# Crossing between stages of a two-layer decoder trunk: passes with a wait for each half, and the last tile transposed into another pair of PSUM banks

## The chip, the cores and the metric

The kernel runs on one core of a Trainium2 chip. The metric is the device time of one execution in microseconds; the median over a few runs counts. The engines are named as the profile names them: PE is TensorE (PEld its weight loads), ACT is ScalarE, DVE is VectorE, POOL is GpSimd, SP is SyncE, which issues most of the DMAs.

## The reference, cut to what matters

A decoder trunk of two layers over 512 tokens with width 1024, all in float32. For each layer i:

```
hn = rms_norm(x, g0);  y = attention_i(hn)          # layer 0 differential, layer 1 native sparse
x = x + rms_norm(y, g1)
hn = rms_norm(x, g2);  u = hn @ w_up                # 1024 -> 5632
c = causal depthwise convolution of u over 3 tokens; gate, val = split(c)
f = (gelu(gate) * val) @ w_down                     # 2816 -> 1024
x = x + rms_norm(f, g3)
x = x + sigmoid(rms_norm(x, g4) @ gate_w) * (p[i] @ proj_w)
```

Native sparse attention compresses keys and values in blocks, attends to the compressed, the selected and the window keys, and adds the three with learned gates. In each sublayer the normalised x is the input of a matrix product, so it must be there transposed (features on the partitions).

## The kernel before, in words

**Splitting.** Every product in float32 is made of three passes of the fast float32r matmul: a value is split into a high part (`_hi`, rounded to float32r) and a low part (`_lo`, the rest), and hi x hi, hi x lo and lo x hi are added up in one PSUM bank. This holds for the weights (`w_hi`, `w_lo`) and for the normalised, transposed x (`nT_hi`, `nT_lo`).

**Weights.** They come in 213 units of 128 x 1024 (512 KB), in the order of use, listed in `PLAN`. For each unit SP loads `w_raw`, ACT copies it to `w_hi` (L356, `w_high`), POOL subtracts to `w_lo` in four parts (L295, `low`), and PE uses it. Each has a ring of four slots. A slot of `w_hi` is free when PE has counted the unit in `units_done`; `w_hi_done` counts the units that ACT has made, `w_lo_done` the quarters that POOL has made. On PE `weights(u)` waits for all quarters of the units before u.

**Tiles.** The 512 tokens are four tiles of 128. PSUM has eight banks of 512 columns, four called A and four called B. A stage that ends with an update of x (attention output, down projection, gate) runs its last units tile by tile (`by_tile`), so that tile 0's x is ready while PE is still at work on the later tiles.

**From one stage to the next.** For the q-th normalisation and for each tile t: ACT makes the sums of squares and the root, DVE writes the normalised tile into the one buffer `xn` in two halves (L785, `prepare`; it waits until the tile before has been transposed), PE transposes it with eight matmuls into two banks (L1179, `transposes`; `xT_banks` names the banks, B[0] and B[1] for every tile), ACT copies them rounded to `nT_hi` (L389) and DVE subtracts to `nT_lo` (L791), which frees the two banks. `xn_done`, `xT_done`, `nhi_done` and `nlo_done` count the halves, 8 for each q. DVE's order at the end is fixed: update of tile 3, `xn` of tile 3, `nT_lo` of tile 2, `nT_lo` of tile 3 (`turns`).

**The crossing.** `transposes(q, 0)` and `(q, 1)` stand inside the last stage's `by_tile`. `cross` is the start of the next stage on PE: it waits for `nT_lo` of tiles 0 and 1 and the first unit's `w_lo`, runs unit 0 on tiles 0 and 1 (`part(0, 0)`), transposes tile 2, waits for `w_lo`, runs unit 1 on tiles 0 and 1, transposes tile 3, runs unit 2 on tiles 0 and 1, then waits for all of `nT_lo` and runs the three units on tiles 2 and 3. It is called five times: into up0 (q = 1), gate0a (2), cmp (3), up1 (4) and gate1a (5). In up0, up1 and cmp a part is `features` over half of the columns, 24 matmuls of 256 columns (L1200) with the weights as stationary operand; in gate0a and gate1a it is `of_tiles` with two tiles, 12 matmuls of 512 columns (L1209) with x as stationary operand. Bank A[n] takes unit n in the first case, bank A[t] tile t in the second.

**After the crossing.** In up0 and up1 units of 24 matmuls follow in a loop. After gate0a and gate1a come two units `ple`, which need `pe_hi` and `pe_lo`: ACT loads `pe_raw` (issued in `embed`, behind the loads of `gains`, which wait for `nlo_done`), copies it and then makes the weights of the ple units.

Of the kernel before, what the change touches and what calls it, by code (L numbers as in the profile page):

```python
# [37 lines left out]
SEQ = 512  # L38
D = 1024
TT = SEQ // P  # L40
KT = D // P
# [26 lines left out]
RING = 4  # L68
# [54 lines left out]
def trunk(nc, x_in, w_in, const_in, gain_in, conv_in, subln_in, lam_in, pos_in, pT_in, w1_in,  # L123
          cpos_in, w2_in, out):
    ctx = ExitStack()
    with ctx:
        def sb(name, shape, dt=F32, on=ctx):
            return on.enter_context(nc.sbuf_tensor(name, shape, dt))
# [3 lines left out]
        nT_hi = sb("nT_hi", [P, KT, SEQ], F32R)  # L132
        nT_lo = sb("nT_lo", [P, KT, SEQ], F32R)
# [88 lines left out]
        A, B = [banks_a[:, n, :] for n in range(4)], [banks_b[:, n, :] for n in range(4)]  # L222
# [17 lines left out]
        S = {n: ctx.enter_context(nc.semaphore(n)) for n in names}  # L240
        block = ctx.enter_context(nc.Block())

        def tok(t):
            return slice(t * P, (t + 1) * P)
# [6 lines left out]

        def xT_banks(q, t):

            return ((A[0], A[1]), (A[2], A[3]), (B[0], B[1]), (B[2], B[3]))[t] if q == 0 else (B[0], B[1])

        def normed(q, t):

            return xn0[:, t, :] if q == 0 else xn[:, :]
# [82 lines left out]
        def _(act):  # L341
# [44 lines left out]
            def nT_high(q, t):  # L386
                for b, bank in enumerate(xT_banks(q, t)):
                    act.wait_ge(S["xT_done"], 8 * q + 2 * t + b + 1)
                    signal(act.activation(nT_hi[:, 4 * b:4 * b + 4, tok(t)],  # L389
                                          bank.rearrange("p (k n) -> p k n", k=4), ACT.Copy),  # L390
                           "nhi_done", 8 * q + 2 * t + b + 1)
# [375 lines left out]
        def _(dve):  # L767
# [20 lines left out]
            def nT_low(q, t):  # L788
                for b, bank in enumerate(xT_banks(q, t)):
                    dve.wait_ge(S["nhi_done"], 8 * q + 2 * t + b + 1)  # L790
                    signal(dve.tensor_tensor(nT_lo[:, 4 * b:4 * b + 4, tok(t)],  # L791
                                             bank.rearrange("p (k n) -> p k n", k=4),
                                             nT_hi[:, 4 * b:4 * b + 4, tok(t)].bitcast(F32), ALU.subtract),
                           "nlo_done", 8 * q + 2 * t + b + 1)
# [378 lines left out]
        def _(pe):  # L1173
            def weights(u):

                pe.wait_ge(S["w_lo_done"], u * PARTS)

            def transpose(dst, src):
                return pe.matmul(dst, src, ident[:, :], start=True, stop=True, is_transpose=True)  # L1179

            def transposes(q, t):

                if q and t:
                    pe.wait_ge(S["nlo_done"], 8 * q + 2 * t)
                for b, bank in enumerate(xT_banks(q, t)):
                    pe.wait_ge(S["xn_done"], 8 * q + 2 * t + b + 1)
                    for k in range(4):
                        m = transpose(bank[:, k * P:(k + 1) * P], normed(q, t)[:, (4 * b + k) * P:(4 * b + k + 1) * P])
                    m.then_inc(S["xT_done"], 1)

            def features(bank, slot, rhs_hi, rhs_lo, part=None, cols=slice(0, SEQ)):


                steps = [(k, pas) for k in range(KT) for pas in range(3)]
                if part is not None:
                    steps = steps[8 * part:8 * part + 8]
                for k, pas in steps:
                    w = (w_hi, w_hi, w_lo)[pas][slot]
                    r = (rhs_hi, rhs_lo, rhs_hi)[pas]
                    m = pe.matmul(bank[:, cols], w[:, k * P:(k + 1) * P], r[:, k, cols], start=(k, pas) == (0, 0),  # L1200
                                  stop=(k, pas) == (KT - 1, 2))
                return m

            def tokens(bank, slot, c, lhs_hi, lhs_lo, kk, t, n_k):

                for pas in range(3):
                    w = (w_hi, w_lo, w_hi)[pas][slot]
                    a = (lhs_hi, lhs_hi, lhs_lo)[pas]
                    m = pe.matmul(bank[:, :], a[:, kk, tok(t)], w[:, c * HALF:(c + 1) * HALF],  # L1209
                                  start=(kk, pas) == (0, 0), stop=(kk, pas) == (n_k - 1, 2))  # L1210
                return m

            def by_unit(U, units, banks, lhs_hi, lhs_lo, n_k, before=None):

                for n in units:
                    weights(U + n + 1)
                    if before:
                        before(n)
                    of_tiles(U, n, range(TT), banks, lhs_hi, lhs_lo, n_k).then_inc(S["units_done"], 1)

            def of_tiles(U, n, tiles, banks, lhs_hi, lhs_lo, n_k):

                for c in range(2):
                    kk = 2 * n + c - (n_k if 2 * n >= n_k else 0)
                    for t in tiles:
                        m = tokens(banks[t], (U + n) % RING, c, lhs_hi, lhs_lo, kk, t, n_k)
                return m

            def by_tile(U, units, banks, lhs_hi, lhs_lo, n_k, within, at, free=None):


                for t in range(TT):
                    if free:
                        free(t)
                    for n in units:
                        if t == 0:
                            weights(U + n + 1)
                        if n == units[at]:
                            within(t)
                        m = of_tiles(U, n, (t,), banks, lhs_hi, lhs_lo, n_k)  # L1240
                        if t == TT - 1:
                            m.then_inc(S["units_done"], 1)
                    if t < TT - 1:
                        m.then_inc(S["tile_done"], 1)

            def cross(U, q, part):


                pe.wait_ge(S["nlo_done"], 8 * q + 4)
                weights(U + 1)  # L1250
                part(0, 0)
                transposes(q, 2)
                weights(U + 2)
                part(1, 0)
                transposes(q, 3)
                weights(U + 3)
                part(2, 0)
                pe.wait_ge(S["nlo_done"], 8 * q + 8)
                for n in range(3):
                    part(n, 1).then_inc(S["units_done"], 1)  # L1260

            def feature_part(U):
                return lambda n, m: features(A[n], (U + n) % RING, nT_hi, nT_lo, cols=slice(256 * m, 256 * m + 256))

            def feature_start(U, q):

                cross(U, q, feature_part(U))
                weights(U + 4)
                features(A[3], (U + 3) % RING, nT_hi, nT_lo).then_inc(S["units_done"], 1)
# [27 lines left out]

            def embed(layer, q, after_q):
                Ua, Up, Ub = PLAN[f"gate{layer}a"], PLAN[f"ple{layer}"], PLAN[f"gate{layer}b"]
                cross(Ua, after_q, lambda n, m: of_tiles(Ua, n, (2 * m, 2 * m + 1), A, nT_hi, nT_lo, KT))  # L1300
                by_unit(Ua, (3,), A, nT_hi, nT_lo, KT)
                pe.wait_ge(S["pelo_done"], layer + 1)
                for half, banks in enumerate((B, A)):
                    weights(Up + half + 1)
                    for t in range(TT):
                        if half:
                            pe.wait_ge(S["sig_done"], 8 * layer + t + 1)
                        for c in range(2):
                            m = tokens(banks[t], (Up + half) % RING, c, pe_hi, pe_lo, c, t, 2)
                    m.then_inc(S["units_done"], 1)  # L1310

                def free(t):
                    pe.wait_ge(S["xhalf_done"], 4 * layer + t + 1)

                def within(t):
                    if q is not None and t >= 2:
                        if t == 2:
                            pe.wait_ge(S["sig_done"], 8 * layer + 6)
                        transposes(q, t - 2)
                by_tile(Ub - 4, range(4, 8), B, nT_hi, nT_lo, KT, within, 2, free)  # L1320
# [4 lines left out]
            for t in range(TT + 1):  # L1325
                if t < TT:
                    transposes(0, t)
                if t:
# [3 lines left out]
                    for n in range(2):  # L1332
                        m = of_tiles(PLAN["v"], n, (t - 1,), A, nT_hi, nT_lo, KT)
# [105 lines left out]
            mlp(0, "up0", 1)  # L1439
            down(0, "down0", 2, 1)  # L1440
            embed(0, 3, 2)


            feature_start(PLAN["cmp"], 3)
            U = PLAN["branch"]
# [15 lines left out]
            for t in range(TT):  # L1461
                m = transpose(A[3][:, tok(t)], gT[:, tok(t)])
# [151 lines left out]
            mlp(1, "up1", 4)  # L1614
            down(1, "down1", 5, 3)
            embed(1, None, 5)


# [103 lines left out]
```

## Time and profile before

| | |
|---|---|
| median of 3 runs | 1533.87 us (1533.52 to 1535.57) |
| the profiled execution, own time | 1532.11 us |
| its span | 1530.3 us |
| PE busy | 1467.9 us (96%) |
| DVE / ACT / POOL busy | 718.1 / 717.3 / 677.4 us |
| granted PE clock, mean | 0.991 of full speed |

The busy time of an engine is the sum over its instructions; PE's matmuls are pipelined, so the pace is read from the starts of neighbouring matmuls and not from their durations. In the timeline a row gives start, length, engine, line, operation, output and inputs, shapes and count, and in brackets how long the engine sat idle before it and what released it. Neighbouring rows of one kind are drawn together: "x8" is eight instructions in one row.

### The profile page before, as it was taken

Reading aid. Unit: us, or ns where it says so; the run is one execution under the profiler, and the core shown is the slowest. Engines: PE = TensorE matmul, PEld = TensorE weight load, DVE = VectorE, ACT = ScalarE, POOL = GpSimd, SP = SyncE. Lnnn points to the kernel's source line nnn. Section 1 sums busy time; section 2 is a strip of 40 time slices with the busy share of each in tenths; the row PEclk is TensorE's granted clock in tenths of the full one; section 3 lists DMA queues with packets and bytes.
Section 4 is the critical chain, followed back from the end, with each engine's and each line's share of the span. In section 5 each row is a group of like instructions: output and inputs, shape, how many; then the busy total and the mean of one; then the engine's idle time right before and its main releaser. Section 6 shows DMA issues by size and latency. Waiting matters only on the chain.

```text
span 1530.3 us, 23460 instructions
## 1 busy us (share of the span) xinstructions
PE 1467.9 (96%) x7566; PEld 1222.1 (80%) x7566; DVE 718.1 (47%) x1256; ACT 717.3 (47%) x1305; POOL 677.4 (44%) x970
## 2 busy tenths in 40 slices
PE   6999979999999999998999999999999999999998
PEld 5877757888888888877978787878788888888876
DVE  5477772644444400335476767673634443410053
ACT  5245543654444413357365656463744444423252
POOL 4634434365656555363420202112455656555452
PEclk9999998999999999999999999999999999999999
DMA  5321111232222222142410101010232222232221
GB/s 206 117 68 55 55 42 58 94 108 98 96 96 96 96 96 97 69 145 78 160 45 13 55 15 41 14 41 28 71 123 96 96 96 96 96 103 91 96 96 55
DMA packets 37131, 126.22 MB, mean 82 GB/s; under 512 B 6096, under 2 KB 6864, under 8 KB 36816
## 3 DMA queue, kind: packets, MB, share of 16 engines
q1 hardware_dynamic: 31824, 115.88, 21.6%
q10 hardware_dynamic: 5248, 9.55, 1.8%
q8 instruction: 37, 0.61, 0.2%
q14 instruction: 22, 0.18, 0.0%
HBM read 123.32 MB, written 2.10 MB: 82 GB/s over the span
## 4 chain that ended last, share of the span: by engine, by line
PE 58%; issue 17%; POOL 16%; DVE 5%; ACT 4%; POOLq 0%; ACTq 0%; DVEq 0%
PE banks_a L1200 22%; POOL w_lo L295 15%; PE banks_b L1209 9%; PE banks_a L1209 8%; PE banks_a L1564 4%; PE banks_b L1200 4%; PE banks_a L1179 4%; PE banks_b L1536 2%; PE banks_b L1356 1%; PE banks_a L1375 1%; DVE nm L938 1%; PE banks_b L1179 1%; PE banks_a L1455 1%; ACT w_hi L356 1%; ACT y L359 0%
## 5 line engine op out<-in xcount | busy, mean ns | idle before, releaser
L295 POOL TENSOR_TENSOR w_lo<-w_raw,w_hi 128x256 fp32r<-128x256 f32 x852 | 647.9, 793 | 776.7 <-ACT w_hi L356 776.6
L1200 PE MATMUL banks_a<-nT_hi,w_hi 128*128 128x512 f32 (+1 forms) x968 | 365.5, 378 | 1.6 <-POOL w_lo L295 1.6
L1200 PE MATMUL banks_a<-nT_lo,w_hi 128*128 128x512 f32 (+1 forms) x968 | 364.0, 376 | 0.0
L1200 PE MATMUL banks_a<-nT_hi,w_lo 128*128 128x512 f32 (+1 forms) x968 | 363.4, 375 | 0.0
L356 ACT ACTIVATE w_hi<-w_raw 128x1024 fp32r<-128x1024 f32 x213 | 225.6, 1061 | 284.5 <-PE banks_b L1209 137.9
L1200 PEld LDWEIGHTS banks_a<-nT_hi,w_hi 128*128 128x128 f32 x968 | 183.7, 190 | 34.2 <-POOL w_lo L295 1.8
L1200 PEld LDWEIGHTS banks_a<-nT_hi,w_lo 128*128 128x128 f32 x968 | 183.6, 190 | 32.0
L1200 PEld LDWEIGHTS banks_a<-nT_lo,w_hi 128*128 128x128 f32 x968 | 183.8, 190 | 31.7
L844 DVE SCALAR_TENSOR_TENSOR y<-banks_a,conv,y 128x511 f32<-128x511 f32 x88 | 66.0, 750 | 220.4 <-ACT y L457 219.9
L457 ACT ACTIVATE y<-banks_a,conv 128x512 f32<-128x512 f32 x88 | 68.6, 779 | 208.8 <-PE banks_a L1200 208.7
L938 DVE TENSOR_REDUCE nm<-banks_b 128x2 f32<-128x256 f32 (+2 forms) x96 | 79.1, 824 | 25.3 <-PE banks_b L1359 12.7
L691 ACT ACTIVATE gp<-banks_b,nm 128x128 f32<-128x128 f32 (+3 forms) x128 | 67.6, 528 | 49.1 <-DVE nm L938 43.4
L1564 PE MATMUL banks_a<-Vg,gpT 128*128 128x128 f32 x640 | 84.6, 280 | 0.0
L802 DVE TENSOR_TENSOR y<-banks_b,g_post 128x512 f32<-128x512 f32 x16 | 11.1, 692 | 143.7 <-ACT y L359 143.7
L1564 PEld LDWEIGHTS banks_a<-Vg,gpT 128*128 128x128 f32 x640 | 76.5, 192 | 0.3
L846 DVE SCALAR_TENSOR_TENSOR y<-banks_a,conv,y 128x510 f32<-128x510 f32 x88 | 65.8, 748 | 12.1
L1209 PE MATMUL banks_a<-w_hi,hT_hi 128*128 128x512 f32 x176 | 69.1, 393 | 0.0
L1209 PE MATMUL banks_a<-w_hi,hT_lo 128*128 128x512 f32 x176 | 68.5, 389 | 0.0
L1209 PE MATMUL banks_a<-w_lo,hT_hi 128*128 128x512 f32 x176 | 68.5, 389 | 0.0
L1209 PE MATMUL banks_b<-w_hi,hT_hi 128*128 128x512 f32 x176 | 68.5, 389 | 0.0
L1209 PE MATMUL banks_b<-w_lo,hT_hi 128*128 128x512 f32 x176 | 68.5, 389 | 0.0
L1209 PE MATMUL banks_b<-w_hi,hT_lo 128*128 128x512 f32 x176 | 68.5, 389 | 0.0
(256 smaller groups left out, 2405.6 us busy)
## 6 DMA issues: line engine op xcount, KB each, us to landing
w_raw<-in_w SPq DMA_DIRECT2D x213, 512.0 KB, 3.2
g_pre<-in_gains ACTq DMA_DIRECT2D x6, 512.0 KB, 6.0
x<-in_x SPq DMA_DIRECT2D x4, 512.0 KB, 9.6
g_post<-in_gains ACTq DMA_DIRECT2D x4, 512.0 KB, 6.9
out<-x SPq DMA_DIRECT2D x4, 512.0 KB, 2.6
pe_raw<-in_pT ACTq DMA_DIRECT2D x2, 512.0 KB, 5.6
w1k<-in_w ACTq DMA_DIRECT2D x1, 1024.0 KB, 4.9
w1v<-in_w ACTq DMA_DIRECT2D x1, 1024.0 KB, 7.0
```

Source lines behind the costliest of these rows:

```text
L295: pool.tensor_tensor(w_lo[slot][:, cols], w_raw[k % RAW][:, cols], w_hi[slot][:, cols].bitcast(F32), ALU.subtract).then_inc(S["w_lo_done"], 1)
L356: act.activation(w_hi[u % RING][:, :], w_raw[u % RAW][:, :], ACT.Copy).then_inc(S["w_hi_done"], 1)
L457: signal(act.activation(dst, bank[:, :], ACT.Identity, bias=conv[:, bass.ds(4 * f + 3, 1)], scale=conv[:, bass.ds(4 * f + 2, 1)]), "aff_do ...
L691: signal(act.activation(gp[:, k % 2, c, 0:n], B[2 * (k % 2) + c][:, 0:n], ACT.Exp, bias=nm[:, qt, c:c + 1], accum_out=sums[:, h % 2, qt, c ...
L844: link(dve.scalar_tensor_tensor(dst[:, 1:SEQ], bank[:, 0:SEQ - 1], conv[:, bass.ds(4 * f + 1, 1)], dst[:, 1:SEQ], ALU.mult, ALU.add))
L846: last = dve.scalar_tensor_tensor(dst[:, 2:SEQ], bank[:, 0:SEQ - 2], conv[:, bass.ds(4 * f, 1)], dst[:, 2:SEQ], ALU.mult, ALU.add)
L938: signal(dve.tensor_reduce(nm[:, qt, :], banks_b[:, b:b + 2, 0:n], AX.X, ALU.max, negate=True), negmax, step + 1)
L1179: return pe.matmul(dst, src, ident[:, :], start=True, stop=True, is_transpose=True)
L1200: m = pe.matmul(bank[:, cols], w[:, k * P:(k + 1) * P], r[:, k, cols], start=(k, pas) == (0, 0), stop=(k, pas) == (KT - 1, 2))
L1209: m = pe.matmul(bank[:, :], a[:, kk, tok(t)], w[:, c * HALF:(c + 1) * HALF], start=(kk, pas) == (0, 0), stop=(kk, pas) == (n_k - 1, 2))
L1536: pe.matmul(B[2 * (k % 2) + c][:, 0:n], Q[h][:, tok(qt)], K[:, c, 0:n], start=K is Kh, stop=False)
L1564: m = pe.matmul(A[c][:, tok(qt)], gpT[:, k % 2, c, kb * P:(kb + 1) * P], Vg[:, kb, HEAD * c:HEAD * c + P], start=kb == 0, stop=kb == qt)
```

## The change

The diff has three parts. `xT_banks` gives tile 3 the banks B[2] and B[3] for q > 0, and `transposes` drops tile 3's wait for `nlo_done` (tiles 0 to 2 keep theirs). `features`, `tokens` and `of_tiles` take a list of passes; with it the three passes no longer alternate within a unit, but each pass runs over the whole part. `cross` calls its parts pass by pass: pass 0 (hi x hi) after waits on `w_hi_done` and `nhi_done`, pass 1 (high weights with `nT_lo`) after `nlo_done`, pass 2 (`w_lo`) after `weights`. The parts on tiles 2 and 3 run in the same order of passes without waits in between.

```diff
         def xT_banks(q, t):
-            return ((A[0], A[1]), (A[2], A[3]), (B[0], B[1]), (B[2], B[3]))[t] if q == 0 else (B[0], B[1])
+            if q == 0:
+                return ((A[0], A[1]), (A[2], A[3]), (B[0], B[1]), (B[2], B[3]))[t]
+            return (B[2], B[3]) if t == TT - 1 else (B[0], B[1])
...
             def transposes(q, t):
-                if q and t:
+                if q and t < TT - 1:
                     pe.wait_ge(S["nlo_done"], 8 * q + 2 * t)
...
-            def features(bank, slot, rhs_hi, rhs_lo, part=None, cols=slice(0, SEQ)):
+            def features(bank, slot, rhs_hi, rhs_lo, part=None, cols=slice(0, SEQ), passes=None):
                 steps = [(k, pas) for k in range(KT) for pas in range(3)]
...
+                if passes is not None:
+                    steps = [(k, pas) for pas in passes for k in range(KT)]
...
-            def tokens(bank, slot, c, lhs_hi, lhs_lo, kk, t, n_k):
-                for pas in range(3):
+            def tokens(bank, slot, c, lhs_hi, lhs_lo, kk, t, n_k, passes=range(3)):
+                for pas in passes:
...
             def cross(U, q, part):
-                pe.wait_ge(S["nlo_done"], 8 * q + 4)
-                weights(U + 1)
-                part(0, 0)
+                def first_tiles(n):
+                    pe.wait_ge(S["w_hi_done"], U + n + 1)
+                    part(n, 0, (0,))
+                    if n == 0:
+                        pe.wait_ge(S["nlo_done"], 8 * q + 4)
+                    part(n, 0, (1,))
+                    weights(U + n + 1)
+                    part(n, 0, (2,))
+                pe.wait_ge(S["nhi_done"], 8 * q + 4)
+                first_tiles(0)
                 transposes(q, 2)
-                weights(U + 2)
-                part(1, 0)
+                first_tiles(1)
                 transposes(q, 3)
-                weights(U + 3)
-                part(2, 0)
+                first_tiles(2)
                 pe.wait_ge(S["nlo_done"], 8 * q + 8)
                 for n in range(3):
-                    part(n, 1).then_inc(S["units_done"], 1)
+                    part(n, 1, (0, 1, 2)).then_inc(S["units_done"], 1)
...
-                cross(Ua, after_q, lambda n, m: of_tiles(Ua, n, (2 * m, 2 * m + 1), A, nT_hi, nT_lo, KT))
+                cross(Ua, after_q, lambda n, m, passes: of_tiles(Ua, n, (2 * m, 2 * m + 1), A, nT_hi, nT_lo, KT,
+                                                       sorted((0, 2, 1)[pas] for pas in passes)))
```

In `tokens` the passes are numbered differently (1 is the one with `w_lo`), which is what the `(0, 2, 1)` translates.

## Rows read from the trace of the kernel before

**Rows 1.** The page: busy time and instructions of the engines; one group of loads.
```profile
PE 1467.9 (96%) x7566; PEld 1222.1 (80%) x7566; DVE 718.1 (47%) x1256; ACT 717.3 (47%) x1305; POOL 677.4 (44%) x970
...
L1200 PEld LDWEIGHTS banks_a<-nT_hi,w_hi 128*128 128x128 f32 x968 | 183.7, 190 | 34.2 <-POOL w_lo L295 1.8
```

**Rows 2.** Waits of PE: us in total, times, longest.
```profile
PE banks_b L1179 <- DVE nT_lo L791: 9.8, 5, 3.8
...
PE banks_a L1200 <- POOL w_lo L295: 1.6, 3, 0.7
```

**Rows 3.** Timeline of PE over the crossing into up0: start, us, what.
```profile
286.21 0.28 PE L1200 MATMUL banks_a<-nT_hi,w_hi 128*128 128x256 f32 x1
...
289.08 1.04 PE L1179 MATMUL banks_b<-ident,xn 128*128 128x128 f32 x8
290.84 0.39 PE L1200 MATMUL banks_a<-nT_hi,w_hi 128*128 128x256 f32 x1 [0.72 <-POOL w_lo L295]
...
295.26 1.09 PE L1179 MATMUL banks_b<-ident,xn 128*128 128x128 f32 x8 [1.29 <-DVE nT_lo L791]
296.11 0.36 PE L1200 MATMUL banks_a<-nT_hi,w_hi 128*128 128x256 f32 x1
```

**Rows 4.** Timeline of POOL and DVE over the same crossing.
```profile
287.01 10.22 POOL L295 TENSOR_TENSOR w_lo<-w_raw,w_hi 128x256 fp32r<-128x256 f32 x12 [1.54 <-ACT w_hi L356]
...
291.69 2.20 DVE L785 SCALAR_TENSOR_TENSOR xn<-x,rinv,g_pre 128x512 f32<-128x512 f32 x2
293.81 1.40 DVE L791 TENSOR_TENSOR nT_lo<-banks_b,nT_hi 128x512 fp32r<-128x512 f32 x2
296.66 1.42 DVE L791 TENSOR_TENSOR nT_lo<-banks_b,nT_hi 128x512 fp32r<-128x512 f32 x2 [1.45 <-ACT nT_hi L389]
```

**Rows 5.** Timeline over the crossing into gate0a: xn of tile 3, unit 2.
```profile
657.99 2.19 DVE L785 SCALAR_TENSOR_TENSOR xn<-x,rinv,g_pre 128x512 f32<-128x512 f32 x2
...
662.41 0.48 PE L1209 MATMUL banks_a<-w_hi,nT_hi 128*128 128x512 f32 x1
```

**Rows 6.** Timeline over the crossing into cmp: xn of tiles 2 and 3.
```profile
716.34 1.93 DVE L785 SCALAR_TENSOR_TENSOR xn<-x,rinv,g_pre 128x512 f32<-128x512 f32 x2
...
718.74 0.36 PE L1200 MATMUL banks_a<-nT_hi,w_hi 128*128 128x256 f32 x1
...
722.83 1.42 DVE L785 SCALAR_TENSOR_TENSOR xn<-x,rinv,g_pre 128x512 f32<-128x512 f32 x2
...
725.62 1.97 PE L1179 MATMUL banks_b<-ident,xn 128*128 128x128 f32 x8 [3.77 <-DVE nT_lo L791]
...
727.24 0.56 PE L1200 MATMUL banks_a<-nT_hi,w_hi 128*128 128x256 f32 x1
...
728.66 0.28 PE L1200 MATMUL banks_a<-nT_hi,w_hi 128*128 128x256 f32 x1
```

**Rows 7.** Crossing into up1: timeline; one stretch, its third last column the granted clock.
```profile
1103.26 2.19 DVE L785 SCALAR_TENSOR_TENSOR xn<-x,rinv,g_pre 128x512 f32<-128x512 f32 x2
...
1106.83 1.35 PE L1179 MATMUL banks_b<-ident,xn 128*128 128x128 f32 x8 [1.97 <-DVE nT_lo L791]
1107.84 0.56 PE L1200 MATMUL banks_a<-nT_hi,w_hi 128*128 128x256 f32 x1
...
1110.96 0.28 PE L1200 MATMUL banks_a<-nT_hi,w_lo 128*128 128x256 f32 x1
...
1109.00:1111.00 2.00, 2.00 (x12) 2.00 (x11) 0.67 (x1) 0.00 (x0) 0.00 (x0) 0.52 0.74 248
```

**Rows 8.** Timeline over the crossing into gate1a: xn of tile 3, unit 2.
```profile
1471.09 2.20 DVE L785 SCALAR_TENSOR_TENSOR xn<-x,rinv,g_pre 128x512 f32<-128x512 f32 x2
...
1475.51 0.47 PE L1209 MATMUL banks_a<-w_hi,nT_hi 128*128 128x512 f32 x1
```

**Rows 9.** Timeline of POOL and PE at the first unit of ple0.
```profile
675.45 2.84 POOL L295 TENSOR_TENSOR w_lo<-w_raw,w_hi 128x256 fp32r<-128x256 f32 x4 [11.93 <-ACT w_hi L356]
...
678.84 0.39 PE L1209 MATMUL banks_b<-w_hi,pe_hi 128*128 128x512 f32 x1
```

More of the change, by code:

```diff
@@ L1219, in by_unit, with of_tiles @@
                     of_tiles(U, n, range(TT), banks, lhs_hi, lhs_lo, n_k).then_inc(S["units_done"], 1)
-            def of_tiles(U, n, tiles, banks, lhs_hi, lhs_lo, n_k):
+            def of_tiles(U, n, tiles, banks, lhs_hi, lhs_lo, n_k, passes=range(3)):
                 for c in range(2):
@@ L1225, in of_tiles @@
                     for t in tiles:
-                        m = tokens(banks[t], (U + n) % RING, c, lhs_hi, lhs_lo, kk, t, n_k)
+                        m = tokens(banks[t], (U + n) % RING, c, lhs_hi, lhs_lo, kk, t, n_k, passes)
                 return m
@@ L1246, in cross @@
             def cross(U, q, part):
-                pe.wait_ge(S["nlo_done"], 8 * q + 4)
-                weights(U + 1)
-                part(0, 0)
+                def first_tiles(n):
[8 more added lines that the diff above has]
+                first_tiles(0)
                 transposes(q, 2)
-                weights(U + 2)
-                part(1, 0)
+                first_tiles(1)
                 transposes(q, 3)
-                weights(U + 3)
-                part(2, 0)
+                first_tiles(2)
                 pe.wait_ge(S["nlo_done"], 8 * q + 8)
                 for n in range(3):
-                    part(n, 1).then_inc(S["units_done"], 1)
+                    part(n, 1, (0, 1, 2)).then_inc(S["units_done"], 1)
             def feature_part(U):
-                return lambda n, m: features(A[n], (U + n) % RING, nT_hi, nT_lo, cols=slice(256 * m, 256 * m + 256))
+                return lambda n, m, passes: features(A[n], (U + n) % RING, nT_hi, nT_lo,
+                                                     cols=slice(256 * m, 256 * m + 256), passes=passes)
             def feature_start(U, q):
```

## The prediction

> **What bounds the kernel now.** I read the page's busy table first, then TensorE's waits, then the timeline of each place where the kernel goes from one stage to the next. TensorE (PE) is busy 96% of the span [rows 1]; what it is not busy for is the only thing to win. Among its waits the two that matter here are "transposes of tile 3 wait for nT_lo", 9.8 us in 5 waits, and "first matmul of a new stage waits for w_lo", 1.6 us in 3 waits of the L1200 stages [rows 2]. Both sit at the five crossings of `cross` (into up0, gate0a, cmp, up1, gate1a, at about 286, 652, 714, 1097 and 1465 us); from there the next stage keeps PE fed, so a microsecond won at a crossing is carried to the end. I found no idle of PE over 0.25 us inside the up and down stages.
>
> The crossing into up0 shows the pattern [rows 3]. Unit 0 on tiles 0 and 1 runs from 286.21 to 289.08: 24 matmuls of 256 columns, 0.12 us each, 2.87 us. Eight transposes follow at 289.08. Then PE sits 0.72 us until unit 1's w_lo is there and restarts at 290.84. Unit 1 takes 2.9 us; then PE sits 1.29 us until 295.26, when tile 3 may be transposed, and restarts with unit 2 at 296.11. What it waits for is the bank: DVE writes tile 3's xn at 291.69 to 293.89, then reads tile 2 out of banks B0 and B1 at 293.81 to 295.21 (nT_lo), and only that lets tile 3's transposes into the same two banks [rows 4].
>
> **The change part by part.**
>
> *Tile 3 into B2 and B3.* It takes the nT_lo wait away. What is late next is xn of tile 3, which nothing in the change moves: it hangs on the last tile's statistics, and its own write waits only for tile 2's transposes. How soon does unit 2 restart after xn's end? Crossing three has the case already, at tile 2: xn ends at 716.34 + 1.93 = 718.27 and the matmul behind the transposes starts at 718.74, 0.47 us later [rows 6]; the first four transposes are done before the second half of xn ends. So the new restart is xn's end + 0.47:
> up0: 293.89 + 0.47 = 294.36 against 296.11, 1.75 us saved [rows 3, 4];
> gate0a: 660.18 + 0.47 = 660.65 against 662.41, 1.76 us [rows 5];
> cmp: 724.25 + 0.47 = 724.72 against 727.24, 2.52 us [rows 6];
> up1: 1105.45 + 0.47 = 1105.92 against 1107.84, 1.92 us [rows 7];
> gate1a: 1473.29 + 0.47 = 1473.76 against 1475.51, 1.75 us [rows 8].
> Sum 9.70 us. Before the restart PE is free in each case: in up0 unit 1 would end near 293.0.
>
> *Pass by pass with a wait for each half.* The first pass (w_hi with nT_hi) needs no w_lo, so unit 1 starts directly behind tile 2's transposes: 0.85 to 1.1 us earlier in four crossings (290.84 against about 289.9 in up0), and unit 0 of cmp 0.3 us earlier. Its third pass comes 1.9 us later, and w_lo was there 0.1 us before the old restart. But nearly all this time is swallowed, for unit 2 restarts by xn, as above. What the passes give beyond that is PE's readiness: in up0 unit 1 would otherwise end at 290.84 + 2.88 = 293.72 and tile 3's first four transposes (0.44 us) at 294.2 instead of 293.94, 0.25 us late. So some 0.2 us of the 1.75 in up0, gate0a and gate1a are theirs, 0.6 us in all; the other 9.1 belong to the banks. The matmuls are the same in number and shape. The waits added are on w_hi and nT_hi, which were there over a microsecond before; behind PE's waits nothing else is queued but PE itself. I take 0, with bounds of 0 and 0.05 us for each of some 8 added waits in 5 crossings, 2 us.
>
> *The wait for tiles 2 and 3, `nlo_done` 8q+8.* DVE now goes from nT_lo of tile 2 straight to tile 3 without its 1.45 us pause: 295.21 + 1.46 = 296.67 in up0 [rows 4]. PE is then in unit 2 until 294.36 + 2.95 = 297.31. The cover is 0.6 us (0.5 in the gate stages, where a part has 12 matmuls of 512 columns). I take 0.
>
> *The clock.* In cmp and up1 the long wait is followed by slow matmuls. After 3.77 us idle the six matmuls from 727.24 to 728.66 take 1.42 us where six at full pace take 0.80; after 1.97 us idle fourteen from 1107.84 to 1110.96 take 3.12 us where 1.76 is the full pace, and the granted clock from 1109 to 1111 is 0.52, the 1.2 GHz level [rows 6, 7]. After the waits of 1.29 us (up0) and of 1.4 us in the gate stages there is no slow stretch. The change leaves in up1 about 0.6 us idle, four transposes, 0.7 us idle; I expect full clock and add 3.12 - 1.76 = 1.36 us. In cmp PE ends unit 1 at 721.85 and finds xn's first half at 723.6, 1.8 us idle, close to the case that fell. If the clock stays up, cmp gains another 1.42 - 0.80 = 0.62 us; if it falls, I price the slow stretch as up1's, 1.36 us. I take the middle of +0.62 and 0.62 - 1.36 = -0.74: -0.1 us.
>
> *What follows gate0a.* The first weights of ple0: w_lo ends at 675.45 + 2.84 = 678.29, and PE asks at 678.84 [rows 9], 0.55 us of cover for 1.76 us of advance. That w_lo hangs on ACT, whose pe_raw load is issued after nlo_done of the crossing, which moves ahead by 1.42 us. 0.55 + 1.42 - 1.76 = 0.21 us left over; bounds 0 and, if the load's landing stays put, 1.21 us lost. I take 0.2 us lost, for the advance may not pass through the queue whole.
>
> Sum: 9.70 + 1.36 - 0.1 - 0.2 = 10.8 us. The profiled execution took 1532.11 us (span 1530.3, 1.8 us around it); 1532.1 - 10.8 = 1521.3. The median of the runs shown is 1533.87, 1.8 us above the profiled one; since times after will be a median too, the forecast is 1533.87 - 10.8 = **1523.1 us**.
>
> **The rivals.**
> A. *The clock falls all the same* in cmp and in up1. For: the half-speed stretch in up1 came after only 1.97 us of idle, so that it may come after 0.6 + 0.7 with transposes between; against: 0.72 + 1.29 us in up0 did not bring it. It takes 1.36 + 0.64 us off: 8.8 us, 1525.1.
> B. *DVE becomes the bound.* PE now arrives at `nlo_done` 8q+8 0.5 to 0.6 us behind DVE. If tile 3's nT_lo operations were stretched as xn is (1.1 us for one of the two instead of 0.7, while GpSimd runs beside them), four in a row would be 1.6 us longer and PE would wait 1.0 us at each crossing, 5 us in all; with the ple0 cover gone too, 1.0 more: gain 4.8 us, 1529.1. Against: nT_lo at 293.81 ran at 0.70 us each beside GpSimd [rows 4].
> C. *Slower: the pass order costs pace.* In the old order of `features` two matmuls in succession use the same stationary operand (w_hi[k] with nT_hi and nT_lo), in the new one none do. If a load stops being hidden, each matmul costs up to the load's own 0.19 us instead of 0.12: 0.07 x 24 matmuls x 6 parts x 3 stages = 30 us, and with the gain taken off 19 us slower, 1553. It decides from 0.025 us per matmul (10.8 / 432). For: nothing in the trace has ever run in this order. Against: there are as many loads as matmuls, 7566 of each [rows 1], and 968 for each of the three passes at the same 190 ns [rows 1], so nothing was shared before. "TensorE: Matmul & The Clock Gate" of the Trainium skill (section "Step-by-step: what each phase is for") says that the load is its own instruction so that one load can serve many matmuls, which would speak against splitting the pair. The same page of the Trainium skill (section "LDWEIGHTS (loading the stationary operand)") gives columns / 1.2 ns for a load, 107 ns for 128 columns, which would still fit under 0.12 us; by that figure the order costs nothing.
> D. *It does nothing.* If xn's second half were late enough to hold PE as long as nT_lo does; the rows have xn 1.4 us before nT_lo's end in all five, so this needs xn to move. 0 us, 1533.9.
>
> **How the numbers follow.** Forecast with the clock saved in up1: 0.76. A 0.13, B 0.05, C 0.03, D 0.03. Own range of the forecast: cmp's clock either way (0.7 us), an added low-clock stretch or one fewer elsewhere (1.4 us, the price of one), the ple0 cover (1.0) and about 1 us of spread between medians (the three runs lie 1533.52 to 1535.57): 1520 to 1526.5. To reach A's far side I extend to 1527.5. A difference of less than 0.2% (3.1 us) can't be told from none. Faster by more: forecast, A, B, 0.94; same: D, 0.03; slower: C, 0.03.
>
> **What would show it.** Right: PE's wait for nT_lo before L1179 gone from all five crossings and a wait for xn of about 0.6 us in its place; the first matmul of unit 2 0.47 us behind xn; no PE wait for w_lo at the crossings; nT_lo of tiles 2 and 3 in one unbroken run of four. Wrong: a wait of PE for nT_lo before a matmul of L1200 or L1209 (B), matmuls of 256 columns further apart than 0.12 us at full clock (C), a granted clock near 0.5 after 1104 us (A), or the stages after a crossing taking back what it gave.

## The result

| | median | runs | ratio to before, 95% interval |
|---|---|---|---|
| before | 1533.52 us | 5 (1531.07 to 1535.57) | |
| changed | 1524.09 us | 5 (1522.84 to 1525.07) | 0.9936 [0.9925, 0.9948] |

The change makes the kernel 9.4 us faster by the medians (forecast 10.8, 1523.1 us); the interval of the ratio is 8.0 to 11.5 us. The profiled execution of the changed kernel took 1524.09 us (span 1522.3), 8.0 us less than that of before.

PE's waits in the changed kernel (us in total, times, longest) answer to [rows 2]:

```profile
PE banks_b L1181 <- DVE xn L787: 4.6, 7, 1.8
...
PE banks_a L1213 <- POOL w_lo L297: 2.5, 1, 2.5
...
PE banks_b L1213 <- POOL w_lo L297: 0.5, 2, 0.3
PE banks_b L1213 <- DVE x L874: 0.5, 1, 0.5
```

The 9.8 us for nT_lo are gone. In their place stand 4.6 us for xn in seven waits, six of them under 0.5 us and one of 1.77 us in cmp. The 2.5 us for w_lo are the very first units of the kernel, at 17.7 us; no wait for w_lo is left in `cross`. Behind gate0a one wait is new, 0.32 us for w_lo, and one has grown: PE's wait for x took 0.16 us before and takes 0.47 us now.

The crossing into up0, PE and DVE (start, us, what), answers to [rows 3, 4]:

```profile
287.72 1.11 PE L1204 MATMUL banks_a<-nT_hi,w_hi 128*128 128x256 f32 x8
288.67 1.12 PE L1204 MATMUL banks_a<-nT_lo,w_hi 128*128 128x256 f32 x8
...
294.33 0.64 PE L1181 MATMUL banks_b<-ident,xn 128*128 128x128 f32 x4
295.45 0.66 PE L1181 MATMUL banks_b<-ident,xn 128*128 128x128 f32 x4 [0.48 <-DVE xn L787]
295.86 0.36 PE L1204 MATMUL banks_a<-nT_hi,w_hi 128*128 128x256 f32 x1
...
293.19 2.21 DVE L787 SCALAR_TENSOR_TENSOR xn<-x,rinv,g_pre 128x512 f32<-128x512 f32 x2
295.32 2.86 DVE L793 TENSOR_TENSOR nT_lo<-banks_b,nT_hi 128x512 fp32r<-128x512 f32 x4
```

xn ends at 293.19 + 2.21 = 295.40, the second four transposes start at 295.45, unit 2 at 295.86: 0.46 us behind xn. nT_lo of tiles 2 and 3 is one run of four and ends at 295.32 + 2.86 = 298.18; PE starts the parts on tiles 2 and 3 at 298.82, 0.64 us later. Eight matmuls of one pass take 288.67 - 287.72 = 0.95 us, 0.119 us each, the pace of before. Unit 2 starts at 660.39, 1102.98 and 1467.52 in gate0a, up1 and gate1a, 0.46 to 0.47 us behind xn each time (the first two are shown). In cmp, where the clock fell, it is 0.95 us (the rows stand with e10).

```profile
657.73 2.19 DVE L787 SCALAR_TENSOR_TENSOR xn<-x,rinv,g_pre 128x512 f32<-128x512 f32 x2
...
660.39 0.47 PE L1213 MATMUL banks_a<-w_hi,nT_hi 128*128 128x512 f32 x1
...
1100.30 2.22 DVE L787 SCALAR_TENSOR_TENSOR xn<-x,rinv,g_pre 128x512 f32<-128x512 f32 x2
...
1102.98 0.36 PE L1204 MATMUL banks_a<-nT_hi,w_hi 128*128 128x256 f32 x1
...
1104.00:1106.00 2.00, 2.00 (x19) 2.00 (x18) 1.26 (x2) 0.00 (x0) 1.22 (x2) 1.00 0.41 156
```

The last row is a stretch behind up1's crossing; its third last column is the granted clock, 1.00 where [rows 7] have 0.52.

PE runs 7566 matmuls in both kernels. I numbered them, took the start of the matmul with the same number in both traces (changed minus before), and differenced it over each piece:

| piece | changed, us | the prediction's term |
|---|---|---|
| start to the first transposes for up0 (before at 274.71, changed at 276.20) | +1.5 | none |
| up0 crossing | -1.75 | -1.75 |
| gate0a crossing | -1.77 | -1.76 |
| ple0 to the end of gate0b | +0.87 | +0.2 |
| cmp crossing | -1.82 | -2.4 |
| up1 crossing | -3.23 | -3.28 |
| gate1a crossing | -1.80 | -1.75 |
| sum | -8.0 | -10.8 |

The first row is not the change: up to there both kernels are the same. It is the end of the differential attention, where PE runs part of the time at half clock. The stretch 217 to 242 us of before, of the changed kernel, and of the changed kernel in another execution (e8):

```profile
217.00:242.00 25.00, 17.96 (x86) 13.76 (x87) 10.93 (x32) 10.37 (x26) 3.63 (x14) 0.73 0.06 22
```
```profile
217.00:242.00 25.00, 18.65 (x79) 13.24 (x80) 10.45 (x28) 9.54 (x25) 3.85 (x15) 0.59 0.07 22
```
```profile
217.00:242.00 25.00, 17.51 (x83) 13.29 (x84) 10.94 (x29) 10.36 (x26) 3.99 (x15) 0.73 0.07 22
```

The granted clock was 0.73, 0.59 and again 0.73 for the same code. The first transposes for up0 start at 276.20 us in one execution of the changed kernel and at 275.29 in the other (e8), and between 274.7 and 277.8 us over all twelve profiles of this study, so this stretch moves from execution to execution. From the first transposes for up0 to the end of the span the change gives 1255.6 - 1246.1 = 9.5 us, which is also what the medians give. I use this "time from there" below beside the medians; it leaves that noise out, but it comes from one execution each.

### The profile page after: what moved, and what is told of

Its sections match the earlier page's. It is cut to its first block, busy times and chain, and to the rows that moved or that the text cites. A ratio compares the mean times of both kernels' runs of the same rounds, so it can differ in the third digit from the quotient of the medians.

```text
span 1522.3 us, 23455 instructions
## 1 busy us (share of the span) xinstructions
PE 1468.9 (96%) x7566; PEld 1221.6 (80%) x7566; DVE 718.9 (47%) x1256; ACT 716.8 (47%) x1305; POOL 677.4 (44%) x970
## 4 chain that ended last, share of the span: by engine, by line
PE 58%; issue 17%; POOL 16%; DVE 5%; ACT 4%; POOLq 0%; ACTq 0%; DVEq 0%
PE banks_a L1204 22%; POOL w_lo L297 15%; PE banks_b L1213 9%; PE banks_a L1213 8%; PE banks_a L1576 4%; PE banks_b L1204 4%; PE banks_a L1181 4%; PE banks_b L1548 2%; PE banks_b L1368 2%; DVE nm L940 1%; PE banks_a L1387 1%; PE banks_a L1467 1%; ACT w_hi L358 1%; ACT y L361 1%; PE banks_b L1551 0%
## 5 line engine op out<-in xcount | busy, mean ns | idle before, releaser
L1204 PE MATMUL banks_a<-nT_hi,w_hi 128*128 128x512 f32 (+1 forms) x968 | 344.5, 377 | 0.0
L1204 PE MATMUL banks_a<-nT_lo,w_hi 128*128 128x512 f32 (+1 forms) x968 | 342.7, 375 | 0.0
L1204 PE MATMUL banks_a<-nT_hi,w_lo 128*128 128x512 f32 (+1 forms) x968 | 342.2, 375 | 0.0
L1204 PEld LDWEIGHTS banks_a<-nT_hi,w_hi 128*128 128x128 f32 x968 | 174.6, 190 | 32.0
L1204 PEld LDWEIGHTS banks_a<-nT_hi,w_lo 128*128 128x128 f32 x968 | 173.7, 189 | 32.1
L1204 PEld LDWEIGHTS banks_a<-nT_lo,w_hi 128*128 128x128 f32 x968 | 173.8, 189 | 31.3
```

## The experiments

All were timed in five rounds or more beside the kernel before on the same chip. "From up0 on" is the span of the profiled execution less the start of the first transposes for up0 (before 1255.6, changed 1246.1, changed again 1246.2).

| kernel | median us | ratio, 95% interval | from up0 on |
|---|---|---|---|
| e1 banks only | 1523.94 | 0.9937 [0.9923, 0.9950] | 1246.0 |
| e2 passes only | 1536.32 | 1.0018 [1.0008, 1.0027] | 1258.3 |
| e3 changed, pe_raw first | 1522.66 | 0.9924 [0.9910, 0.9937] | 1244.7 |
| e4 changed, fill | 1521.54 | 0.9914 [0.9901, 0.9928] | 1242.2 |
| e5 before, kept busy | 1531.11 | 0.9981 [0.9972, 0.9990] | 1252.7 |
| e6 changed, nT_lo twice | 1528.13 | 0.9965 [0.9952, 0.9979] | 1249.6 |
| e7 changed, fill and pe_raw first | 1520.76 | 0.9912 [0.9899, 0.9926] | 1241.2 |
| e8 changed again | 1523.17 | 0.9932 [0.9919, 0.9946] | 1246.2 |
| e9 passes only, kept busy | 1531.11 | 0.9983 [0.9974, 0.9992] | 1252.9 |
| e10 changed, kept busy in cmp | 1522.01 | 0.9927 [0.9913, 0.9941] | 1244.3 |

**e8: the changed kernel once more, with nothing edited,** to see how far its own figures scatter.

> The changed kernel again, to be compared with the others on this chip: 1523 to 1525 us, 9 to 10 us faster than before.

Measured: 1523.17 us against 1524.09, and 1246.2 against 1246.1 us from up0 on. The last figure is the steadier one, though not in every piece: between ple0 and gate0b, e10 loses 0.4 us less than the changed kernel, with the same instructions up to that point.

**e1 and e2: each half of the change alone.** e1 is the kernel before with

```diff
-            return ((A[0], A[1]), (A[2], A[3]), (B[0], B[1]), (B[2], B[3]))[t] if q == 0 else (B[0], B[1])
+            if q == 0:
+                return ((A[0], A[1]), (A[2], A[3]), (B[0], B[1]), (B[2], B[3]))[t]
+            return (B[2], B[3]) if t == TT - 1 else (B[0], B[1])
...
-                if q and t:
+                if q and t < TT - 1:
```

and e2 is the changed kernel with these lines as before.

> The kernel before with only the bank part of the change: tile 3 goes to B2 and B3 and its transposes drop the wait for nlo_done; the passes stay as before. Theory (the banks carry nearly all of it): about 0.6 us less gain than the full change, plus up to 0.4 us of w_lo wait kept at the start of cmp; some 8 to 9 us faster than before, PE's wait for nT_lo gone, its 1.6 us of w_lo waits kept, unit 2 in up0 restarting some 0.25 us later behind xn than in the changed kernel. Rival (the halves' waits carry half of the gain): 4 to 5 us faster only.

> The changed kernel with tile 3 back in B0 and B1 and its wait for nlo_done back: only the pass-by-pass order with its split waits is left. Theory: unit 1 ends 0.8 to 1.1 us earlier and the wait for nT_lo grows by the same amount (9.8 to about 13 us in total), so the time stays that of before, within 0.5 us. In up1 the longer wait may cost more slow clock, up to 0.4 us. Rival C (the order costs pace): matmuls of 256 columns more than 0.12 us apart at full clock and a time above before. Rival (the passes carry half of the gain): 4 us faster.

Measured: the banks alone give all of it, 1523.94 us against 1524.09 and 1523.17. In the crossings into up0, gate0a and gate1a e1 advances by 1.53, 1.55 and 1.61 us against 1.75, 1.77 and 1.80, so the passes' share of 0.2 us each is there as predicted. It is given back between ple0 and gate0b, where e1 loses 0.25 us and the changed kernel 0.87. The whole of e1, 9.9 us by the medians, is more than the 8 to 9 us that I expected. PE in e1, up0: unit 1 still waits for w_lo, and tile 3's transposes run without a pause.

```profile
292.24 0.39 PE L1202 MATMUL banks_a<-nT_hi,w_hi 128*128 128x256 f32 x1 [0.71 <-POOL w_lo L297]
295.21 1.03 PE L1181 MATMUL banks_b<-ident,xn 128*128 128x128 f32 x8
```

The passes alone are not free as I expected, but 2.5 us slower by the medians and 2.7 us from up0 on. The pace within a pass is 0.12 us at full clock (eight matmuls from 302.59 to 303.55), so it is not rival C. e2's timeline of PE at tile 3's transposes in up0, gate0a and up1, and a stretch behind each:

```profile
298.20 1.97 PE L1179 MATMUL banks_b<-ident,xn 128*128 128x128 f32 x8 [2.26 <-DVE nT_lo L791]
...
302.59 1.12 PE L1202 MATMUL banks_a<-nT_hi,w_lo 128*128 128x256 f32 x8
303.55 1.12 PE L1202 MATMUL banks_a<-nT_hi,w_hi 128*128 128x256 f32 x8
...
666.05 1.28 PE L1179 MATMUL banks_b<-ident,xn 128*128 128x128 f32 x8 [2.52 <-DVE nT_lo L791]
...
1112.45 1.09 PE L1179 MATMUL banks_b<-ident,xn 128*128 128x128 f32 x8 [2.88 <-DVE nT_lo L791]
```
```profile
299.00:302.00 3.00, 3.00 (x18) 3.00 (x16) 1.38 (x2) 1.19 (x2) 1.14 (x2) 0.57 0.62 220
667.00:670.00 3.00, 3.00 (x9) 2.42 (x8) 1.38 (x2) 0.94 (x2) 1.00 (x2) 0.50 0.60 209
1112.00:1115.00 3.00, 2.55 (x22) 2.56 (x23) 1.52 (x3) 1.20 (x2) 1.74 (x3) 1.00 0.47 165
```

Before, the crossing into up0 had two waits, 0.72 and 1.29 us, and kept the full clock. The passes join them into one of 2.26 us, and the clock falls to 0.5 behind it. The pieces of e2 against before, from the starts of the matmuls:

| crossing | clock before | clock in e2 | e2 loses (+) or gains (-), us |
|---|---|---|---|
| up0 | kept | fell | +1.55 |
| gate0a | kept | fell | +1.63 |
| ple0 to the end of gate0b | kept | kept | -0.65 |
| cmp | fell | fell | +0.12 |
| up1 | fell | kept | -1.49 |
| gate1a | kept | fell | +1.55 |

So in this execution the clock falls at four crossings instead of two, and each fall costs about 1.5 us. The other piece, behind gate0a, has no fall; there PE comes later in e2 and finds x and w_lo ready, where before it waited 0.16 and 0.21 us. Three crossings lose the clock with one longer wait; up1 keeps it behind 2.88 us, where it fell before behind 1.97 us. That one piece is worse than two is therefore the outcome of these three crossings and no rule.

**e5, e9 and e10: is it PE's own idle that lowers the clock?** In front of tile 3's transposes PE runs matmuls whose result nobody reads: 30 in cmp and 15 in up1 (e5, on the kernel before), 30 in cmp and 15 in each other crossing (e9, on e2), 13 in cmp (e10, on the changed kernel).

```diff
+                for _ in range({3: 30, 4: 15}.get(q, 0)):
+                    pe.matmul(B[2][:, 0:256], w_hi[(U + 1) % RING][:, 0:P], nT_hi[:, 0, 0:256], start=True, stop=True)
                 transposes(q, 3)
```

> The kernel before with idle filled: ahead of tile 3's wait for nT_lo PE runs 30 matmuls of 256 columns in cmp and 15 in up1 whose result (bank B2) nobody reads; output unchanged. Theory (PE's own idle makes the clock fall in cmp and up1, and the fallen clock costs 1.4 us each): the tile 3 transposes start when they did, no half-speed stretch in cmp nor up1, some 2.5 us faster than before although PE does 45 matmuls more. Rival (the clock falls there for another reason): the half-speed stretches stay and the time is that of before or worse.

> The passes alone (as in e2) with PE's longer idle filled: ahead of tile 3's wait for nT_lo 15 matmuls of 256 columns (30 in cmp) whose result in bank B2 nobody reads; output unchanged. Theory (the pass order itself is free, and e2 is slower only because its one long wait per crossing lets the clock fall more often): no half-speed stretch at any crossing, 5 us faster than e2 and some 2.5 us faster than before, as e5. Rival (the order costs pace or a wait of its own): faster than e2 but not faster than before.

> The changed kernel with 13 such matmuls in cmp alone, in the 1.8 us in which PE waits for xn of tile 3. Theory (in cmp the fallen clock is what separates the changed kernel from the forecast there): no half-speed stretch in cmp, unit 2 restarts 0.47 us behind xn, 1.0 to 1.4 us faster than the changed kernel. Rival (the fall comes from the whole stretch around the crossing and not from this wait): it stays.

Measured: e5 is 2.7 us faster than before, with 45 matmuls more. In cmp and up1 the wait shrinks to 0.18 and 0.19 us, and the granted clock stays at 1.00 behind it (the first row is cmp's):

```profile
728.77 1.09 PE L1179 MATMUL banks_b<-ident,xn 128*128 128x128 f32 x8 [0.18 <-DVE nT_lo L791]
```
```profile
727.00:731.00 4.00, 3.82 (x33) 3.62 (x32) 2.42 (x5) 1.41 (x3) 0.00 (x0) 1.00 0.23 90
1108.00:1112.00 4.00, 3.81 (x33) 3.61 (x33) 1.85 (x3) 1.20 (x2) 1.86 (x3) 1.00 0.54 178
```

e9 is 5.2 us faster than e2, and faster than its own before (0.9983). The comparison for the pass order is e5, which fills the idle time in front of its two falls but has the old order: both have a median of 1531.11 us, and they take 1252.7 and 1252.9 us from up0 on. With the clock kept, the pass order costs nothing. The same stretches as in e2 now read

```profile
299.00:302.00 3.00, 3.00 (x27) 3.00 (x26) 1.38 (x2) 1.20 (x2) 1.30 (x2) 1.00 0.61 191
667.00:670.00 3.00, 3.00 (x15) 2.49 (x14) 0.44 (x1) 0.00 (x0) 0.00 (x0) 1.00 0.71 254
```

27 matmuls in 3 us instead of 18. In e10 the clock is kept in cmp, the one crossing where it fell in the changed kernel. The time from up0 on is 1.8 us shorter. In the cmp crossing itself e10 gains 1.35 us: unit 2 restarts 0.47 us behind xn instead of 0.95, and the other 0.87 us are its matmuls at full pace. The remaining 0.4 us come between ple0 and gate0b, before the edit acts. By the medians it is 1.2 to 2.1 us. The changed kernel in cmp and then e10, with the granted clock behind:

```profile
721.66 1.42 DVE L787 SCALAR_TENSOR_TENSOR xn<-x,rinv,g_pre 128x512 f32<-128x512 f32 x2
...
722.47 1.91 PE L1181 MATMUL banks_b<-ident,xn 128*128 128x128 f32 x8 [1.77 <-DVE xn L787]
724.03 0.56 PE L1204 MATMUL banks_a<-nT_hi,w_hi 128*128 128x256 f32 x1
...
722.50:726.00 3.50, 3.50 (x17) 3.49 (x18) 3.26 (x5) 2.09 (x3) 0.00 (x0) 0.51 0.28 108
```
```profile
722.62 1.32 PE L1181 MATMUL banks_b<-ident,xn 128*128 128x128 f32 x8 [0.24 <-DVE xn L787]
...
722.00:726.00 4.00, 3.76 (x31) 3.32 (x30) 3.90 (x6) 2.26 (x3) 0.20 (x1) 1.00 0.52 147
```

For e5 and e9, with 11 executions each, the medians bear out that PE's idle time costs the clock. For e10 the proof is weaker, because the same wait in cmp did not always bring the fall. It is 1.76 to 1.79 us long in the changed kernel, e8, e1 and e3, where the clock fell, and just as long in e4 and e6, where it stayed up. Both of these are described below; e6 differs from the changed kernel on DVE alone. PE in e6, and the stretch behind:

```profile
723.07 1.32 PE L1185 MATMUL banks_b<-ident,xn 128*128 128x128 f32 x8 [1.79 <-DVE xn L787]
```
```profile
723.00:726.50 3.50, 3.42 (x28) 3.19 (x29) 3.36 (x7) 2.26 (x3) 0.25 (x1) 1.00 0.47 140
```

**e3: what is given back behind gate0a.** On ACT the load of pe_raw for layer 0 moves ahead of the loads of gains:

```diff
             output_norm(1, 1, "down0", FT, 2)
+            load_ple(0)
             gains(3, 2)
```

> The changed kernel with one move on ACT: the pe_raw load of layer 0 is issued ahead of the loads of gains and their wait, right behind nT_hi of tile 3. Theory (the 0.9 us given back between gate0a and cmp hang on the landing of pe_raw, which moved ahead by 1.1 us only): pe_raw lands over 2 us earlier, PE's waits of 0.32 us for w_lo and 0.47 us for x at ple0 go, 0.9 us faster than the changed kernel. Rival (the loss is due to x and the sigmoids, whatever pe_raw does): both waits stay, no gain.

Measured: 1.4 us less from up0 on, 0.5 to 1.4 by the medians. The late use of pe_raw is what held it. ACT before, in the changed kernel, then in e3:

```profile
664.46 0.34 ACTq L397 DMA_DIRECT2D g_pre<-in_gains  x1
...
673.22 1.06 ACT L483 ACTIVATE pe_hi<-pe_raw 128x1024 fp32r<-128x1024 f32 x1 [9.73 <-DMA pe_raw<-in_pT]
```
```profile
662.79 0.34 ACTq L399 DMA_DIRECT2D g_pre<-in_gains  x1
...
664.22 1.87 ACTq L483 DMA_DIRECT2D pe_raw<-in_pT  x1
672.08 1.06 ACT L485 ACTIVATE pe_hi<-pe_raw 128x1024 fp32r<-128x1024 f32 x1 [10.75 <-DMA pe_raw<-in_pT]
```
```profile
661.30 0.34 ACTq L480 DMA_DIRECT2D pe_raw<-in_pT  x1
...
666.23 1.06 ACT L489 ACTIVATE pe_hi<-pe_raw 128x1024 fp32r<-128x1024 f32 x1 [4.96 <-DMA pe_raw<-in_pT]
```

Issued first, pe_raw is used 4.9 us after its issue, against 7.9 us as the last of four, and it is issued 2.9 us earlier. PE's waits of 0.32 and 0.47 us are gone, and with them a wait of 0.20 us for w_lo at 693.48. The kernel before had two of these three as well (0.16 us for x, 0.21 us for w_lo), which is why e3 gains more than the 0.9 us that had been given back.

**e4 and e7: filling the new wait.** Pass 0 of unit 2 goes between the halves of tile 3's transposes:

```diff
                 for b, bank in enumerate(xT_banks(q, t)):
+                    if b and between:
+                        between()
...
-                transposes(q, 3)
-                first_tiles(2)
+                transposes(q, 3, lambda: first(2))
+                second(2)
+                third(2)
```

(`first`, `second` and `third` are the three passes of `first_tiles` with their waits.) e7 adds e3's move, and in cmp puts pass 0 ahead of the transposes and pass 1 between them.

> The changed kernel with pass 0 of unit 2 placed between the two halves of tile 3's transposes. Theory (what PE waits for is now the second half of xn, 0.49 us idle in four crossings and more in cmp, while nT_lo of tiles 2 and 3 has some 0.5 us of cover): the idle of 0.49 us is filled in up0, gate0a, up1 and gate1a, 0.4 us each, 1.6 to 2 us faster than the changed kernel, with PE then reaching the wait for all of nT_lo at just about the time it is done. Rival (the cover is thinner than computed): the idle moves to a wait for nT_lo before the parts on tiles 2 and 3, and the time stays.

> The changed kernel with both additions: pass 0 of unit 2 between the two halves of tile 3's transposes (in cmp pass 0 ahead of them and pass 1 between them) and the pe_raw load issued ahead of the loads of gains. Theory: the gains of the two (1.4 us and 2.5 us by their medians) add, 1520.0 to 1520.8 us; clock kept in cmp. Rival (they use the same cover behind gate0a): no better than the better of the two, 1521.5.

Measured: e4 is 1.6 to 2.6 us faster than the changed kernel by the medians and 3.9 us from up0 on. PE in e4, up0 (in e4's own time, in which tile 3's xn ends at 296.78 and nT_lo at 299.56):

```profile
295.71 0.65 PE L1181 MATMUL banks_b<-ident,xn 128*128 128x128 f32 x4
296.12 1.20 PE L1206 MATMUL banks_a<-nT_hi,w_hi 128*128 128x256 f32 x8
297.15 0.60 PE L1181 MATMUL banks_b<-ident,xn 128*128 128x128 f32 x4
```

The idle between the halves is gone. The crossings into up0 and up1 gain 0.5 us each, those into gate0a and gate1a 0.26 us each, 1.5 us together, a little under the 1.6 to 2 us expected. The rest of the 3.9 us is not the filled idle: 1.6 us come in cmp, where the clock held in this execution although PE still waited 1.76 us, and 0.9 us between ple0 and gate0b, where pe_raw was used 11.5 us behind xn instead of 12.2. Whether the edit brings either is not shown. The waits list no wait for nT_lo, but in these four crossings the parts on tiles 2 and 3 start 0.05 to 0.06 us behind the end of nT_lo, the same distance as in e6, where PE does wait for it: the cover is used up, and DVE and PE arrive together.

e7 is the fastest kernel of the study, 1520.76 us and 1241.2 from up0 on; the two gains (1.4 and 3.9) add up to a little more than the 4.9 measured. Its median lies only 0.8 us under e4's, with overlapping intervals. In cmp its fill leaves waits of 0.81 us for xn and 0.60 us for nT_lo, and the clock held.

**e6: how much cover DVE has.** In each crossing tile 2's nT_lo is computed twice:

```diff
+                    if q and t == TT - 2:
+                        link(dve.tensor_tensor(nT_lo[:, 4 * b:4 * b + 4, tok(t)],
+                                               bank.rearrange("p (k n) -> p k n", k=4),
+                                               nT_hi[:, 4 * b:4 * b + 4, tok(t)].bitcast(F32), ALU.subtract))
```

> The changed kernel with tile 2's two nT_lo operations done twice in each crossing, 1.4 us more for DVE between xn and nT_lo of tile 3; same values. Theory (after the change DVE has 0.4 to 0.6 us of cover at PE's wait for all of nT_lo): PE waits 0.8 to 1.0 us for nT_lo before the first part on tiles 2 and 3 in each of the five crossings, 4 to 5 us slower than the changed kernel. Rival (much cover, as PE still hangs on xn): same time.

Measured: 5.0 us slower by the medians than the changed kernel beside it (e8), 3.4 us from up0 on. PE waits for nT_lo in all five crossings, 3.7 us together:

```profile
PE banks_a L1208 <- DVE nT_lo L797: 2.1, 3, 0.7
PE banks_a L1217 <- DVE nT_lo L797: 1.6, 2, 0.8
```

The waits view counts from the end of PE's last matmul, so I take the cover from the starts. In e6 a part starts 0.06 us behind the end of nT_lo. In the changed kernel it starts 0.64 us behind it in up0 and up1 and 0.52 us in gate0a and gate1a, so the cover is 0.6 and 0.5 us. In cmp it is the same when the clock is kept (0.65 us in e10). These four crossings lose 0.9 to 1.1 us each in e6; cmp gains 0.4 us, because the clock held there.

The profiled execution of e6 is the fastest of its five, 1526.63 us against a median of 1528.13, and that is the 1.5 us between 3.4 and 5.0.

## Why the prediction was right

*Tile 3 into other banks: right, to a few hundredths.* The restart 0.47 us behind xn, read from tile 2 in cmp, was measured at 0.46 to 0.47 in four crossings. In cmp it was 0.95 us, as the transposes too ran at the low clock. e1 shows that the banks alone carry the change: predicted were 9.1 of 9.7 us for the banks, measured is the whole gain.

*Pass by pass: right that it moves only PE's readiness, wrong to call its price nothing in every setting.* The 0.6 us that I gave it appear in the crossings and vanish behind gate0a. By itself it makes the kernel slower (e2), through the clock, which I had only as rival A and only for cmp and up1: it gathers two short waits into a long one, and the clock fell at three more crossings and at one fewer. In the changed kernel no such harm shows; the waits left in up0, gate0a, up1 and gate1a are under 0.5 us each, and the clock is kept there. Rival C, a cost of the order itself, did not come: 0.119 us per matmul, and e9 is as fast as e5. On the rule of the Trainium skill (page "TensorE: Matmul & The Clock Gate", section "Step-by-step: what each phase is for") that one load may serve many matmuls: the trace shows no gain from having the same stationary operand twice in succession. Both kernels make 7566 loads for 7566 matmuls, and the pace is 0.12 us in both orders.

*`nlo_done` 8q+8: right.* Cover predicted 0.6 us, and 0.5 in the gate stages; measured 0.58 and 0.46 (0.64 and 0.52 less the 0.06 us of e6). Rival B did not come.

*The clock.* up1: predicted 1.36 us saved, and the whole crossing came out at 3.23 against 3.28. In cmp I took the middle between kept and fallen; it fell in both profiles of the changed kernel, and the crossing gave 1.82 us, which is the fallen branch (2.52 - 0.74 = 1.78). That is 0.6 us of the miss. The price of the fall, taken from up1 as 1.36 us, is 1.35 us in cmp between the changed kernel and e10. Why the clock falls behind this wait is not known: it held behind the same wait in e4 and e6, so which branch the profile showed was partly chance, and the middle was a fair value.

*Behind gate0a: the term was mis-sized.* I wrote 0.2 us with a bound of 1.21; measured 0.87. The 1.42 us of advance arrived at the issue and not at the use. The load of g_pre moved from 664.46 to 662.79 and the use of pe_raw from 673.22 to 672.08. In both numbers 0.25 us are the place of the crossing in the trace (xn of tile 3 ends at 660.18 and at 659.93), which leaves 1.42 us for the issue and 0.89 us for the use. With 0.55 us of cover and 1.77 us of advance on PE, 0.55 + 0.89 - 1.77 = -0.33 us, and PE waits 0.32 us for w_lo. The sentence that the advance may not pass through the queue whole was right, the 0.2 us for it too small. Then PE's wait for x grew from 0.16 to 0.47 us: ACT's sigmoids stand behind the same pe_hi, and I had counted only the weights. e3 takes both away.

Sum: 10.8 - 0.6 (cmp) - 0.7 (behind gate0a) = 9.5, as measured from up0 on. The 8.0 us between the two profiled executions hold 1.5 us of slower attention that is no part of the change. The absolute forecast of 1523.1 us missed the median of 1524.09 by 1.0 us, less than the 1.4 us of the gain (10.8 against 9.4), because the median of before was itself 0.35 us lower in the five executions than in the three shown; that part is luck.

## What to carry to other kernels

Where a transfer through a buffer waits for the buffer and not for its data, another buffer is worth the difference to what is late next, and a place elsewhere in the same trace may already show how soon the engine restarts behind it. Before joining or splitting waits of TensorE, look at the granted clock behind each: a fall cost about 1.5 us here, as much as the waits themselves. With the waits joined it appeared at three crossings and vanished at one, so only a trace can say. When PE is made earlier, follow every chain that does not move with it whole, a load issued last behind others first of all.

## What the runs showed of the hardware that was not expected

- Matmuls whose result is thrown away made the kernel faster: 45 of them, 2.7 us less (e5), with the clock at its upper level where it had fallen before.
- The length of a wait alone does not decide on the clock: it fell behind 1.97 us (before, up1), 2.26 us (e2, up0) and 1.77 us (changed, cmp), and stayed up behind 2.88 us (e2, up1) and behind 1.76 and 1.79 us in cmp (e4, e6). What decides between them stays open.
- The same code ran the end of the differential attention at a mean granted clock of 0.73 in one execution of the changed kernel and 0.59 in another, and reached up0 0.9 us apart. Over the twelve profiles up0 begins within 3.1 us, while the executions of one kernel lie 1.2 to 4.5 us apart. That most of their scatter comes from there is likely but not shown.
